# The heads of the mLSTM: spread, logits and denominators' products between the feature tiles of the filling weight products

## The chip, the cores and the metric

The kernel runs on one core of a Trainium2 chip. The metric is the device time of one execution in microseconds; lower is better. The kernel before takes 2386.91 us (median of 3 executions, 2385.71 to 2389.31).

## What is computed

Two transformer blocks over 512 tokens of width 1024, in float32. The first block is a feed-forward part, a mixer, and a feed-forward part. Its mixer projects the normalised input by one weight matrix (29 chunks of 128 output columns here) and feeds two recurrent branches: four heads of a gated linear recurrence (hgrn2) and four heads of the mLSTM. The second block has attention heads in place of the mixer. The change touches only the mLSTM heads, whose reference is (cut):

```
D = where(causal, b[..., :, None] - b[..., None, :] + ic[..., None, :], -inf)
m_t = maximum(a, max(D, axis=-1))
P = einsum("bhtd,bhsd->bhts", qc, kc) * exp(D - m_t[..., None])
num = inter[..., None] * einsum("bhtd,bhdv->bhtv", qc, C) + einsum("bhts,bhsv->bhtv", P, vc)
den = inter * einsum("bhtd,bhd->bht", qc, n) + sum(P, axis=-1)
h = num / maximum(abs(den), exp(-m_t))[..., None]
```

The kernel computes this without chunks: for each head the whole causal half of the 512 x 512 matrix, as ten blocks of 128 x 128 in 1280 columns.

## The kernel before

Every weight chunk (128 x 1024 float32) is loaded by the sync engine's DMA queue into one of three buffers, split by GpSimd into a high and a low part (L323, L325) and multiplied by TensorE: `mm3` (L360 to L362) makes three products of 512 columns (high by high, low by high, high by low), and `pe_dense` (L365) does so for each of the eight feature tiles, 24 products for a chunk, into one bank of PSUM. Each engine runs its own program in order, and semaphores with counts join them.

In the mixer `pe_gated_mixer` writes out TensorE's order by hand. `fill(i)` is one weight chunk; such fills stand between the steps of the recurrences so that TensorE has work while the other engines do theirs. The mLSTM part starts after `fill(23)`. TensorE turns the values (`pe_turn`, L491) into banks 0 to 3, and ScalarE copies these to SBUF (L1337). For each head h there are then:

- `logits(h)`: a spread (L618), which multiplies a selector of 4 rows by the running maximum, 512 columns into bank 3, and four products of keys by queries (L620) with 64 contracted rows and 512, 384, 128 and 256 columns, into banks 0 to 2. The spread releases ScalarE (`decay(h)`, L1351, four exponentials into the buffer E[h % 2]); the last product releases VectorE (`weigh(h)`: L1863 multiplies, L1867 and L1869 mask).
- `values(h)`: waits for the masked E, then four products of values by E (L631, 1280 columns, into bank 6), which VectorE copies out (L1873), and ten products of E by a column of ones for the denominators (L637). After that `den_done` is signalled.
- `pe_head_sums` (L742): four products by a column of ones over the squares that ScalarE makes of the head's output (L1278).

Each float32 product that isn't split into high and low parts shows as two records in the trace, so ten products of denominators are 20 records, four logits are 8.

TensorE's order before is: turn, fill 12, logits 0, fill 13, values 0 (with the denominators), logits 1, fill 14, values 1, sums, logits 2, fill 15, values 2, sums, logits 3, fill 24, values 3, sums, fill 25, sums, fill 26, fill 27, spreads for the norm. A fill waits for ScalarE's copy of the fill two before it (`take`, L1255 and L1257), since two banks alternate. ScalarE's order is: take 12, decay 0, take 13, decay 1, squares, take 14, decay 2, squares, take 15, decay 3, the Silu of the hgrn gate (L1368), take 24, squares, four casts (L1356), squares, takes 25 and 26. VectorE's order is: weigh 0, copy 0, weigh 1, copy 1, weigh 2, copy 2, weigh 3, then the gating of the four hgrn heads (L1841, L1845), copy 3, and the chain of small steps for the denominators and the norm (L1892 and on).

Of the kernel before, what the change touches and what calls it, by code (L numbers as in the profile page):

```python
# [10 lines left out]
ACT = mybir.ActivationFunctionType  # L11
# [3 lines left out]
P = 128  # L15
T = 512
NT = T // P
D = 1024
KD = D // P
# [5 lines left out]
HEADS = 4  # L25
# [20 lines left out]
C_SEL = C_RESET + T  # L46
# [192 lines left out]
def tile(t, i):  # L239
    return t[:, i * T:(i + 1) * T]  # L240
# [46 lines left out]
def fill_bank(tile_number):  # L287
    return 4 + FILL.index(tile_number) % 2
# [75 lines left out]

def pe_dense(k, name, i, bank):  # L365

    pe = k.nc.tensor
    n, hi, lo = k.pair(name, i)
    pe.wait_ge(k.w_split, 2 * n + 2)
    for t in range(KD):  # L370
        m = mm3(pe, k.ps[bank], hi, lo, slice(t * P, (t + 1) * P), tile(k.uhi, t), tile(k.ulo, t), t == 0, t == KD - 1)
    m.then_inc(k.w_used, 1)

# [166 lines left out]
def pe_gated_mixer(k):  # L540
# [7 lines left out]

    def fill(i):
        idx = FILL.index(i)  # L550
        if idx < 2:
            pe.wait_ge(k.qf_taken, 5 + idx)
        else:
            wait_filled(k, pe, FILL[idx - 2])
        pe_dense(k, "mix_in", i, fill_bank(i))

# [49 lines left out]

    def logits(h):

        rows = slice((h % 2) * ML_QK, (h % 2 + 1) * ML_QK)
        qh, kh = tile(g.mqk, h // 2)[rows, :], tile(g.mqk, 2 + h // 2)[rows, :]  # L610
        if h:
            pe.wait_ge(k.decayed, h)
            pe.wait_ge(k.weighed, h)
        else:
            pe.wait_ge(k.turned_copied, 9)
            pe.wait_ge(k.seq_dve, 7)
            pe.wait_ge(k.conv_silu, 1)
        pe.matmul(k.ps[3], k.const[0:HEADS, C_SEL + h * P:C_SEL + (h + 1) * P], g.M, start=True, stop=True).then_inc(k.m_spread, 1)  # L618
        for (i, t0, n, c) in ML_CAUSAL:
            m = pe.matmul(k.psum[:, c:c + n], kh[:, i * P:(i + 1) * P], qh[:, t0:t0 + n], start=True, stop=True)  # L620
        m.then_inc(k.qk_product, 1)

    def values(h):
        E, sum_w = g.E[h % 2], k.ps[7][:, 128:128 + HEADS * NT]
        pe.wait_ge(k.masked, h + 1)
# [7 lines left out]
        m.then_inc(k.hd_out, 1)  # L633
        for j in range(NT):
            for i in range(j + 1):
                c = ML_BASE[i] + (j - i) * P
                m = pe.matmul(sum_w[:, h * NT + j:h * NT + j + 1], E[:, c:c + P], k.cst(C_ONE, 1), start=i == 0, stop=i == j)  # L637
        m.then_inc(k.den_done, 1)

# [57 lines left out]
    pe_turn(k, g.mv_in, 0, 4 * NT)  # L697
    fill(12)
    logits(0)
    fill(13)  # L700
    values(0)
    logits(1)
    fill(14)
    values(1)
    pe_head_sums(k, HEADS)
    logits(2)
    fill(15)
    values(2)
    pe_head_sums(k, HEADS + 1)
    logits(3)  # L710
    fill(24)
    values(3)
    pe_head_sums(k, HEADS + 2)
    fill(25)
    pe_head_sums(k, HEADS + 3)
# [516 lines left out]
def act_gated_mixer(k):  # L1232
    act, g, m = k.nc.scalar, Gated(k), k.misc
    H = HEADS
# [102 lines left out]
    act.copy(g.mv, k.psum[:, 0:4 * T]).then_inc(k.turned_copied, 1)  # L1337
    take(12)

# [18 lines left out]
    decay(0)  # L1358
    take(13)
    decay(1)  # L1360
    squares(H, tile(g.ml_out, 0))
    take(14)
    decay(2)
    squares(H + 1, tile(g.ml_out, 1))
    take(15)
    decay(3)
    act.wait_ge(k.filled, FILL.index(15) + 1)
    act.activation(g.hgate, g.hgate, ACT.Silu).then_inc(k.gates_done, 1)  # L1368
    take(24, ACT.Sigmoid)
    squares(H + 2, tile(g.ml_out, 2))  # L1370
    for h in range(H):
        pair_hi(h, tile(g.hg_out, h))
    squares(H + 3, tile(g.ml_out, 3))
    take(25, ACT.Sigmoid)
    take(26, ACT.Sigmoid)
# [956 lines left out]
```

## Time and profile before

| | |
|---|---|
| median of the runs | 2386.91 us |
| the profiled execution's own time | 2389.54 us |
| its span, first to last instruction | 2387.9 us |
| TensorE matmul busy | 2314.7 us, 97% |
| VectorE / ScalarE / GpSimd busy | 816.6 / 448.7 / 1320.8 us |
| mean granted TensorE clock | 0.986 |

The span is the profiled execution from the first to the last instruction; the 1.6 us between it and the execution's own time lie around it. The granted clock is 1.00 where TensorE runs at 2.4 GHz and 0.50 where it runs at 1.2 GHz. The mLSTM heads lie between 578 and 657 us of the span. A row of the timeline has its start, its duration (a matmul's modelled end lies beyond the start of the next one, so the distance between starts is what counts), engine, line, operation and count.

### The profile page before, as it was taken

The numbers are of one execution on the slowest core, as the hardware profiler recorded it, in microseconds if no ns is written. First come the engines' busy times: TensorE is split into PE (matmuls) and PEld (weight loads), VectorE is DVE, ScalarE is ACT, GpSimd is POOL, SyncE is SP. The second block draws the span as 40 slices with busy tenths as digits, with TensorE's granted clock in tenths as the row PEclk, the third lists the DMA queues.
The fourth block names the chain that finished last, engine by engine and source line by source line (L and its number), as shares of the span: only waits on it lengthen the run. The fifth ranks groups of instructions, "written<-read, shape, count | busy, mean of one in ns | idle before, by whom it ended". The sixth has DMA issues, their size and how long they took to land.

```text
span 2387.9 us, 26080 instructions
## 1 busy us (share of the span) xinstructions
PE 2314.7 (97%) x11060; PEld 1905.6 (80%) x11060; DVE 816.6 (34%) x838; ACT 448.7 (19%) x736; POOL 1320.8 (55%) x772
## 2 busy tenths in 40 slices
PE   6999999999999999999999999999988999999999
PEld 6888888887778888888888888777656788888887
DVE  2323104884244333104323104420567632333013
ACT  3111003323222111003111002111268121111011
POOL 4666665634156666665666665566114656666654
PEclk9999999999799999999999999999899999999999
DMA  4333332211123333332333332223000223333322
GB/s 158 97 97 97 97 97 71 80 54 54 36 80 97 97 97 97 97 97 72 97 97 97 97 97 84 85 88 99 27 1 1 73 86 97 98 97 100 104 86 82
DMA packets 55580, 201.05 MB, mean 84 GB/s; under 512 B 6409, under 2 KB 6537, under 8 KB 55337
## 3 DMA queue, kind: packets, MB, share of 16 engines
q1 hardware_dynamic: 53712, 193.62, 26.4%
q10 hardware_dynamic: 1752, 5.77, 0.6%
q8 instruction: 88, 1.44, 0.3%
q14 instruction: 28, 0.22, 0.0%
HBM read 197.27 MB, written 2.10 MB: 83 GB/s over the span
## 4 chain that ended last, share of the span: by engine, by line
PE 88%; DVE 6%; ACT 3%; issue 1%; DMA 1%; POOL 1%; ACTq 0%; DVEq 0%; POOLq 0%
PE psum L360 19%; PE psum L361 18%; PE psum L362 18%; PE psum L420 7%; PE psum L422 7%; PE psum L421 7%; PE psum L400 1%; PE psum L565 1%; ACT junk L1145 1%; DVE x L1629 1%; PE psum L1069 1%; PE psum L620 1%; PE psum L1071 1%; PE psum L1070 1%; PE psum L458 1%
## 5 line engine op out<-in xcount | busy, mean ns | idle before, releaser
L325 POOL TENSOR_TENSOR w_lo<-w_raw,w_hi 128x1024 fp32r<-128x1024 f32 (+1 forms) x365 | 891.3, 2442 | 30.5
L323 POOL TENSOR_SCALAR w_hi<-w_raw 128x1024 fp32r<-128x1024 f32 (+1 forms) x365 | 388.4, 1064 | 909.9 <-PE psum L362 659.9
L360 PE MATMUL psum<-u_hi,w_hi 128*128 128x512 f32 (+1 forms) x2072 | 795.3, 384 | 10.8 <-DVE work L1977 4.7
L361 PE MATMUL psum<-u_hi,w_lo 128*128 128x512 f32 (+1 forms) x2072 | 789.9, 381 | 0.0
L362 PE MATMUL psum<-u_lo,w_hi 128*128 128x512 f32 (+1 forms) x2072 | 789.4, 381 | 0.0
L360 PEld LDWEIGHTS psum<-u_hi,w_hi 128*128 128x128 f32 x2072 | 392.6, 189 | 90.2 <-issue 7.8
L362 PEld LDWEIGHTS psum<-u_lo,w_hi 128*128 128x128 f32 x2072 | 392.4, 189 | 74.5
L361 PEld LDWEIGHTS psum<-u_hi,w_lo 128*128 128x128 f32 x2072 | 392.8, 190 | 73.6 <-issue 0.7
L420 PE MATMUL psum<-w_hi,hidden_hi 128*128 128x512 f32 x800 | 311.8, 390 | 1.0 <-DVE work L1836 1.0
L421 PE MATMUL psum<-w_lo,hidden_hi 128*128 128x512 f32 x800 | 311.2, 389 | 0.0
L422 PE MATMUL psum<-w_hi,hidden_lo 128*128 128x512 f32 x768 | 298.8, 389 | 0.0
L1666 DVE TENSOR_TENSOR scratch<-scratch,psum 128x512 f32<-128x512 f32 x88 | 60.5, 688 | 586.8 <-PE psum L362 586.8
L1668 DVE TENSOR_TENSOR hidden_lo<-scratch,hidden_hi 128x512 fp32r<-128x512 f32 x88 | 239.4, 2720 | 60.8 <-ACT hidden_hi L1224 60.8
L420 PEld LDWEIGHTS psum<-w_hi,hidden_hi 128*128 128x128 f32 x800 | 150.2, 188 | 32.6 <-DVE work L1836 1.4
L421 PEld LDWEIGHTS psum<-w_lo,hidden_hi 128*128 128x128 f32 x800 | 150.2, 188 | 31.4 <-issue 0.2
L422 PEld LDWEIGHTS psum<-w_hi,hidden_lo 128*128 128x128 f32 x768 | 144.1, 188 | 30.0
L1224 ACT CAST hidden_hi<-scratch 128x512 fp32r<-128x512 f32 x88 | 55.0, 625 | 479.4 <-DVE scratch L1666 479.4
L1222 ACT ACTIVATE scratch<-psum 128x512 f32<-128x512 f32 x88 | 52.6, 598 | 345.9 <-PE psum L362 345.9
L1632 DVE SCALAR_TENSOR_TENSOR x<-psum,x 128x1024 f32<-128x1024 f32 x12 | 14.6, 1218 | 240.2 <-PE psum L422 240.2
L341 POOL TENSOR_SCALAR work<-work,misc 128x512 f32<-128x512 f32 (+3 forms) x32 | 34.2, 1086 | 110.3 <-DVE misc L2109 110.3
L1611 DVE RECIPROCAL misc<-misc 128x1 f32<-128x1 f32 x12 | 1.9, 156 | 243.2 <-ACT misc L1155 243.2
L1145 ACT ACTIVATE junk<-x 128x1024 bf16<-128x1024 f32 x28 | 29.5, 1055 | 272.5 <-DVE x L1632 261.3
(269 smaller groups left out, 1735.6 us busy)
## 6 DMA issues: line engine op xcount, KB each, us to landing
w_raw<-in_ffn_in SPq DMA_DIRECT2D x176, 512.0 KB, 3.5
w_raw<-in_ffn_out SPq DMA_DIRECT2D x88, 512.0 KB, 3.5
w_raw<-in_proj_in SPq DMA_DIRECT2D x34, 512.0 KB, 3.5
w_raw<-in_mix_in SPq DMA_DIRECT2D x29, 512.0 KB, 3.5
w_raw<-in_embed SPq DMA_DIRECT2D x10, 512.0 KB, 3.5
w_raw<-in_mix_out SPq DMA_DIRECT2D x8, 512.0 KB, 3.4
w_raw<-in_branch SPq DMA_DIRECT2D x8, 512.0 KB, 3.6
w_raw<-in_proj_out SPq DMA_DIRECT2D x8, 512.0 KB, 3.5
```

Of the source, the lines that this page charges most:

```text
L323: pool.tensor_scalar(hi, raw, 1.0, 1.0, ALU.mult, ALU.mult).then_inc(k.w_split, 1)
L325: pool.tensor_tensor(lo, raw, hi.bitcast(F32), ALU.subtract).then_inc(k.w_split, 1)
L360: pe.matmul(out, hi[:, cols], xhi, start=first, stop=False)
L361: pe.matmul(out, lo[:, cols], xhi, start=False, stop=False)
L362: return pe.matmul(out, hi[:, cols], xlo, start=False, stop=last)
L420: pe.matmul(bank, xhi(kk)[:, tokens], hi[:, cols], start=kk == 0, stop=False)
L421: pe.matmul(bank, xhi(kk)[:, tokens], lo[:, cols], start=False, stop=False)
L422: return pe.matmul(bank, xlo(kk)[:, tokens], hi[:, cols], start=False, stop=last)
L1145: act.activation(k.junk[:, :], x_tile(k, i), ACT.Square, accum_out=k.x_ss[:, i:i + 1]).then_inc(k.x_squared, 1)
L1224: act.copy(tile(k.hhi, i), hm).then_inc(k.hid_hi, 1)
L1666: dve.tensor_tensor(hm, sg, k.ps[CHUNK_BANK[(2 * i + 1) % 4]], ALU.mult).then_inc(k.multiplied, 1)
L1668: dve.tensor_tensor(tile(k.hlo, i), hm, tile(k.hhi, i).bitcast(F32), ALU.subtract).then_inc(k.hid_lo, 1)
```

## The change

`pe_dense` takes a function that is called after each feature tile but the last. `logits` and the denominators' products are cut up and issued from it: one spread or one product of the logits in a gap, and one column of denominators (1, 2, 3 or 4 products) in a gap. The logits of head h+1 and the denominators of head h now stand in the same fill, logits first. The values' products and the sums stay whole, between fills. Everything moves one fill earlier for the logits: those of head 0 stand in fill 12, not after it.

```
-def pe_dense(k, name, i, bank):
+def pe_dense(k, name, i, bank, between=None):
     for t in range(KD):
         m = mm3(pe, k.ps[bank], hi, lo, slice(t * P, (t + 1) * P), tile(k.uhi, t), tile(k.ulo, t), t == 0, t == KD - 1)
+        if between and t < KD - 1:
+            between(t)

-    def logits(h):
+    def logits(h, t):
-        if h:
-            pe.wait_ge(k.decayed, h)
-            pe.wait_ge(k.weighed, h)
-        else:
-            pe.wait_ge(k.turned_copied, 9)
-            pe.wait_ge(k.seq_dve, 7)
-            pe.wait_ge(k.conv_silu, 1)
-        pe.matmul(k.ps[3], k.const[0:HEADS, C_SEL + h * P:C_SEL + (h + 1) * P], g.M, start=True, stop=True).then_inc(k.m_spread, 1)
+        if t == 0:
+            if h:
+                pe.wait_ge(k.decayed, h)
+                pe.wait_ge(k.weighed, h)
+            else:
+                pe.wait_ge(k.turned_copied, 9)
+                pe.wait_ge(k.seq_dve, 7)
+                pe.wait_ge(k.conv_silu, 1)
+            pe.matmul(k.ps[3], k.const[0:HEADS, C_SEL + h * P:C_SEL + (h + 1) * P], g.M, start=True, stop=True).then_inc(k.m_spread, 1)
-        for (i, t0, n, c) in ML_CAUSAL:
+        elif t <= NT:
+            i, t0, n, c = ML_CAUSAL[t - 1]
             m = pe.matmul(k.psum[:, c:c + n], kh[:, i * P:(i + 1) * P], qh[:, t0:t0 + n], start=True, stop=True)
-        m.then_inc(k.qk_product, 1)
+            if t == NT:
+                m.then_inc(k.qk_product, 1)

+    def denominators(h, j):
...
+        for i in range(j + 1):
+            c = ML_BASE[i] + (j - i) * P
+            m = pe.matmul(sum_w[:, h * NT + j:h * NT + j + 1], E[:, c:c + P], k.cst(C_ONE, 1), start=i == 0, stop=i == j)
+        if j == NT - 1:
+            m.then_inc(k.den_done, 1)
+    def between_heads(h):
+        def between(t):
+            if h + 1 < HEADS and t <= NT:
+                logits(h + 1, t)
+            if t >= 3:
+                denominators(h, t - 3)
+        return between

-    fill(12)
-    logits(0)
-    fill(13)
+    fill(12, lambda t: logits(0, t))
     values(0)
-    logits(1)
-    fill(14)
+    fill(13, between_heads(0))
     values(1)
     pe_head_sums(k, HEADS)
-    logits(2)
-    fill(15)
+    fill(14, between_heads(1))
     values(2)
     pe_head_sums(k, HEADS + 1)
-    logits(3)
-    fill(24)
+    fill(15, between_heads(2))
     values(3)
     pe_head_sums(k, HEADS + 2)
+    fill(24, between_heads(3))
     fill(25)
```

ScalarE's order follows: decay 0, take 12, decay 1, squares, take 13, decay 2, squares, take 14, decay 3, squares, take 15, the gate's Silu, the four casts, squares, take 24, takes 25 and 26. VectorE's and GpSimd's programs are unchanged.

## Rows read from the trace of the kernel before

**Rows 1.** The chain that ended last, by engine (shares of the span).
```profile
PE 88%; DVE 6%; ACT 3%; issue 1%; DMA 1%; POOL 1%; ACTq 0%; DVEq 0%; POOLq 0%
```

**Rows 2.** Windows: stretch, its length, busy us by engine, granted clock, DMA.
```profile
core 0: us, PE busy (x) PEld busy (x) DVE busy (x) ACT busy (x) POOL busy (x), PEclk, DMA share, GB/s
587.20:592.80 5.60, 5.60 (x25) 4.61 (x25) 2.25 (x3) 0.00 (x0) 0.34 (x1) 1.00 0.30 94
597.20:601.90 4.70, 4.70 (x11) 2.18 (x10) 0.00 (x0) 2.30 (x5) 0.00 (x0) 0.71 0.36 112
601.90:609.40 7.50, 7.50 (x26) 6.00 (x25) 2.25 (x3) 0.00 (x0) 0.00 (x0) 0.73 0.00 0
614.70:626.90 12.20, 12.20 (x35) 8.04 (x35) 2.25 (x3) 2.30 (x5) 0.00 (x0) 0.72 0.10 39
632.20:644.40 12.20, 12.20 (x35) 7.90 (x35) 3.46 (x5) 6.26 (x7) 0.00 (x0) 0.72 0.10 39
648.80:656.80 8.00, 8.00 (x33) 6.58 (x34) 3.61 (x7) 1.87 (x3) 0.00 (x0) 0.79 0.23 68
```

**Rows 3.** TensorE in order of time, heads 0 and 1.
```profile
583.51 0.39 PE L362 MATMUL psum<-u_lo,w_hi 128*128 128x512 f32 x1
583.83 1.12 PE L618 MATMUL psum<-work,const 4*128 4x512 f32 x2
584.88 2.42 PE L620 MATMUL psum<-work 64*128 64x512 f32 x8
587.23 0.50 PE L360 MATMUL psum<-u_hi,w_hi 128*128 128x512 f32 x1
587.57 0.40 PE L361 MATMUL psum<-u_hi,w_lo 128*128 128x512 f32 x1
...
592.81 2.32 PE L631 MATMUL psum<-work 128*128 128x512 f32 x8
594.96 2.29 PE L637 MATMUL psum<-const,work 128*128 128x1 f32 x20
597.18 1.12 PE L618 MATMUL psum<-work,const 4*128 4x512 f32 x2
...
601.90 0.79 PE L360 MATMUL psum<-u_hi,w_hi 128*128 128x512 f32 x1
...
609.40 2.32 PE L631 MATMUL psum<-work 128*128 128x512 f32 x8
```

**Rows 4.** TensorE in order of time: a head's sums, and a fill after sums.
```profile
613.71 1.03 PE L742 MATMUL psum<-const,scratch 128*128 128x1 f32 x8
614.67 0.69 PE L618 MATMUL psum<-work,const 4*128 4x512 f32 x1
...
657.63 0.49 PE L360 MATMUL psum<-u_hi,w_hi 128*128 128x512 f32 x1
657.95 0.40 PE L361 MATMUL psum<-u_hi,w_lo 128*128 128x512 f32 x1
```

**Rows 5.** TensorE's weight loads around the logits of head 0.
```profile
583.83 0.29 PEld L618 LDWEIGHTS psum<-work,const 4*128 4x128 f32 x2 [0.35 <-issue]
587.23 0.19 PEld L360 LDWEIGHTS psum<-u_hi,w_hi 128*128 128x128 f32 x1 [0.33 <-issue]
```

**Rows 6.** The turned values: TensorE's first product of fill 12, ScalarE's copy.
```profile
578.18 0.48 PE L360 MATMUL psum<-u_hi,w_hi 128*128 128x512 f32 x1
578.47 1.87 ACT L1337 COPY work<-psum 128x2048 f32<-128x2048 f32 x1 [2.12 <-PE psum L491]
```

**Rows 7.** VectorE's weighing of head 0: first and last operation.
```profile
587.42 1.49 DVE L1863 SCALAR_TENSOR_TENSOR work<-work,psum 128x1280 f32<-128x1280 f32 x1 [16.39 <-PE psum L620]
589.42 0.28 DVE L1869 TENSOR_TENSOR work<-work,const 128x128 f32<-128x128 f32 x1
```

**Rows 8.** ScalarE's Silu of the gate, VectorE from the first hgrn remainder to the last head's copy.
```profile
636.43 1.91 ACT L1368 ACTIVATE work<-work 128x2048 f32<-128x2048 f32 x1
646.30 2.50 DVE L1845 TENSOR_TENSOR hidden_hi<-work,hidden_hi 128x512 fp32r<-128x512 f32 x1 [4.88 <-ACT hidden_hi L1356]
651.13 0.68 DVE L1873 COPY work<-psum 128x512 f32<-128x512 f32 x1
```

More of the change, by code:

```diff
@@ L547, in pe_gated_mixer, with fill @@
         pe_dense(k, "mix_in", FIRST[n], CHUNK_BANK[n % 4])
-    def fill(i):
+    def fill(i, between=None):
         idx = FILL.index(i)
@@ L554, in fill @@
             wait_filled(k, pe, FILL[idx - 2])
-        pe_dense(k, "mix_in", i, fill_bank(i))
+        pe_dense(k, "mix_in", i, fill_bank(i), between)
     def level(n):
@@ L605, in hgrn_out @@
         m.then_inc(k.hd_out, 1)
-    def logits(h):
+    def logits(h, t):
         rows = slice((h % 2) * ML_QK, (h % 2 + 1) * ML_QK)
         qh, kh = tile(g.mqk, h // 2)[rows, :], tile(g.mqk, 2 + h // 2)[rows, :]
-        if h:
-            pe.wait_ge(k.decayed, h)
-            pe.wait_ge(k.weighed, h)
-        else:
-            pe.wait_ge(k.turned_copied, 9)
-            pe.wait_ge(k.seq_dve, 7)
-            pe.wait_ge(k.conv_silu, 1)
-        pe.matmul(k.ps[3], k.const[0:HEADS, C_SEL + h * P:C_SEL + (h + 1) * P], g.M, start=True, stop=True).then_inc(k.m_spread, 1)
-        for (i, t0, n, c) in ML_CAUSAL:
+        if t == 0:
[9 more added lines that the diff above has]
+            i, t0, n, c = ML_CAUSAL[t - 1]
             m = pe.matmul(k.psum[:, c:c + n], kh[:, i * P:(i + 1) * P], qh[:, t0:t0 + n], start=True, stop=True)
-        m.then_inc(k.qk_product, 1)
+            if t == NT:
+                m.then_inc(k.qk_product, 1)
     def values(h):
-        E, sum_w = g.E[h % 2], k.ps[7][:, 128:128 + HEADS * NT]
+        E = g.E[h % 2]
         pe.wait_ge(k.masked, h + 1)
@@ L633, in values @@
         m.then_inc(k.hd_out, 1)
[L634 to L638, printed above, removed]
+    def denominators(h, j):
+        E, sum_w = g.E[h % 2], k.ps[7][:, 128:128 + HEADS * NT]
+        for i in range(j + 1):
[10 more added lines that the diff above has]
+        return between
     def rows():
@@ L1337, in act_gated_mixer @@
     act.copy(g.mv, k.psum[:, 0:4 * T]).then_inc(k.turned_copied, 1)
-    take(12)
     act.wait_ge(k.cols_done, 1)
@@ L1358, in act_gated_mixer @@
     decay(0)
-    take(13)
+    take(12)
     decay(1)
     squares(H, tile(g.ml_out, 0))
-    take(14)
+    take(13)
     decay(2)
     squares(H + 1, tile(g.ml_out, 1))
+    take(14)
+    decay(3)
+    squares(H + 2, tile(g.ml_out, 2))
     take(15)
-    decay(3)
     act.wait_ge(k.filled, FILL.index(15) + 1)
     act.activation(g.hgate, g.hgate, ACT.Silu).then_inc(k.gates_done, 1)
-    take(24, ACT.Sigmoid)
-    squares(H + 2, tile(g.ml_out, 2))
     for h in range(H):
@@ L1373, in act_gated_mixer @@
     squares(H + 3, tile(g.ml_out, 3))
+    take(24, ACT.Sigmoid)
     take(25, ACT.Sigmoid)
```

## The prediction

> **What bounds the kernel now.** I read the chain of waits first. TensorE holds 88% of it [rows 1], so nearly all time is TensorE's, and a change of its order counts fully where it never idles. The question is then what its time in this stage is made of. I listed its timeline from the turn of the values (578 us) to the last sums (657 us): it has no idle time there, every row starts where the one before ends [rows 3]. So neither ScalarE nor VectorE sets the pace, and nothing that they do sooner brings anything. Then I asked for the granted clock of each stretch [rows 2]. This is what the reader is to see: fill 13 runs at 1.00 and takes 5.6 us, but logits 1 run at 0.71 and fill 14 at 0.73, the stretches of heads 2 and 3 at 0.72, and fill 25 with the sums before it at 0.79. The clock sits at 1.2 GHz in part of each, without any idle time of TensorE. What ran before each fall is alike: the denominators' products (one moving column each), the sums (one column), the spread (4 rows) and the start of the logits (64 rows), in one unbroken piece. After logits 0, which stand alone between two fills, it does not fall.
>
> **The gain: the clock.** Logits and fill at full clock are head 0's: from the spread at 583.83 to the values at 592.81, 8.98 us. Head 1's, from 597.18 to 609.40, are 12.22 us [rows 3]. That costs 3.24 us. By the clock alone it would be 4.7 x 0.29 + 7.5 x 0.27 = 3.39 us [rows 2]; the real loss is 0.956 of it. Over all six stretches: 1.36 + 2.03 + 12.2 x 0.28 x 2 + 8.0 x 0.21 = 11.9 us [rows 2], times 0.956 is **11.4 us**. That is all that a steady clock can give.
>
> Will the clock hold? In the new order the longest piece without a wide product of 128 rows is the sums (0.96 us [rows 4]) and then, after a tile of 0.68 us, the spread; every other narrow piece is at most a 512-column product of logits or 0.9 us of denominators, with 0.68 us of weight product on either side. In the old order denominators, sums, spread and the first logits ran together before the falls in heads 2 and 3, 2.22 + 0.96 + 1.05 us and more [rows 3, 4]. Around logits 0, with a fill on either side of 3.4 us of spread and logits, no fall came. I take it that the clock holds in the heads, with some doubt, since wide products fill only 5.45 of each 11 to 12 us.
>
> **The price: changes of rows.** The weight loads show it [rows 5]. Before a product with 4 or 64 rows after one of 128, and before one of 128 after one of 64, the load starts only when the array is free: 0.35 and 0.33 us without a load, and the load and its product start together. In numbers [rows 3]: 1280 columns of values with 128 rows take 594.96 - 592.81 = 2.15 us, the same 1280 columns of logits take 587.23 - 584.88 = 2.35, so 0.20 more. The spread's 512 columns should be 0.86 and take 1.05, 0.19 more. Going in costs 0.09 (583.51 + 0.227 = 583.74, start at 583.83), and the fill's first product after it takes 0.34, not 0.227, 0.11 more. Altogether 0.09 + 0.19 + 0.20 + 0.11 = 0.59 us for three changes, 0.20 each. Before there are three changes in a head: fill to spread, spread to logits, logits to fill. After there are ten, two around each of the five single pieces. Seven more, in four heads, 28 x 0.20 = **5.6 us**. (A fill's ordinary pace of 0.227 is fill 13: 24 products in 5.58 us less 0.12 for its slow start.)
>
> The Trainium skill says (TensorE: Matmul & The Clock Gate, Part 3, The mechanism) that TensorE pulls a weight load ahead of running products when its row group doesn't conflict or it goes into the background buffer. By that, the loads between changes of rows should mostly hide. The trace shows them hidden from 128 rows to 128 rows only [rows 5]; by the rule the 5.6 us would be near nothing, and the forecast some 5 us lower. I follow the rows; the rule is a rival below.
>
> **The price: denominators in pieces.** A one-column product costs its weight load, 2.22 us for 20 = 0.111 each [rows 3]; that stays, wherever it stands. But after the last the fill's load has nothing to hide under: the first product of a fill after sums takes 0.32 us, not 0.227 [rows 4], so 0.10. Before, denominators were followed by other narrow work. Now there are 16 pieces, and two more sums go straight into a fill: 18 x 0.10 = 1.8 us, with a little at the entry **2.0 us**. Bounds: nothing, if the load hides, and 18 x 0.2 = 3.6, if it is priced as a change of rows.
>
> **The waits.** (1) The spread of head 0 waits for ScalarE's copy of the turned values, which ends at 578.47 + 1.87 = 580.34 [rows 6]. Before, all of fill 12 lay over it. Now only the first tile does: from 578.18 three products, to about 578.97. With 0.1 us to the release the spread starts near 580.45, so TensorE idles **1.4 us**, with the other seven tiles queued behind it. Its own other conditions are long met. (2) Values 0 wait for the mask. From the first operation of weighing to the end of the last, 587.42 to 589.70 [rows 7], and 0.27 us before it from the last logits' stream end (587.15): 2.55 us, 2.65 with the release. After the last logits piece there are three tiles, 0.09 + 0.34 + 8 x 0.227 = 2.25 us. **0.4 us** idle; before, a whole fill covered it. For heads 1 to 3 the three tiles have denominators 1 (part), 2 and 3 between them, 1.5 us more, and it is covered. (3) The idle 1.4 us stands between the turn, one tile and the narrow spread. A fall of the clock there would cost like fill 25's, 8.0 x 0.21 x 0.956 = 1.6 us [rows 2]; I give it a half: **0.8 us**. Bounds for (1): 0.9 to 2, by what the release costs; for (2) 0 to 1.
>
> **Costed at nothing.** The decay of a head follows its spread by the same distance, and the weighing waits for the last logits anyway. Take 12 behind decay 0 is late by nothing, as fill 14 needs it only a head later. The Silu now starts after take 15, that is after fill 15: about 0.8 + 1.28 (table load, the time from the decay's end to 636.43) + 1.91 = 4 us after it [rows 8]. Then VectorE has the gating and the copy of head 3: two operations of 0.68 us and what took from 646.30 to 651.81 [rows 8], 6.9 us, and ScalarE's squares 0.6: about 12 us after fill 15. The last sums, before fill 26, come after values 3 (2.15), sums (0.96), fill 24 with denominators (5.45 + 2.2 + 0.5) and fill 25 (5.45), some 17 us after it. Slack 5 us, and if it were gone it would be paid one for one. The weights come with the same order of chunks and more time between them. What follows (root, diagonals, spreads, output products) hangs on fills 26 and 27 as before and moves with them.
>
> **The sum.** -11.4 + 5.6 + 2.0 + 1.4 + 0.4 + 0.8 = -1.2 us. On the profiled execution: 2389.54 - 1.2 = 2388.3. This one execution lies 2.6 us above the median 2386.91, so the forecast in medians is **2385.7, say 2386 us**: a large gain eaten nearly whole. Its own range, by the bounds of the terms, is 2383 to 2389.
>
> **Rivals.**
>
> *A, the clock still falls in the heads.* Wide products fill only about half of each fill now. Against it: around logits 0 the mix was the same and the clock held. For it: here the sums stand right before it, and such a mix goes on for 30 us on end. If it falls as often as before, the gain is nothing and all prices stay: -0 + 7.6 + 1.8 + 0.8 = +10, 2397 us. If it falls once or twice, at 1.6 to 3.3 us each, 2387 to 2392. The point from which it decides against the change is at about one fall of 1.6 us above my sum. This is the one on the slower side.
>
> *B, the changes of rows hide.* This is what the rule in the Trainium skill (the page and section above) would make of it. Then 28 changes cost nothing, -11.4 + 2.0 + 2.6 = -6.8, 2380 us. Every change of rows in this stretch speaks against it [rows 5].
>
> *C, another engine is late for the new order.* VectorE's gating collides with GpSimd's split, as at 646.30, where a remainder took 2.50 us in place of 0.68 [rows 8], and copy 3 is late for the last sums. It would need 5 us of it, three collisions: 2388 to 2391.
>
> **How the numbers follow.** My forecast 0.58; A in full 0.06, A in part 0.18; B 0.12; C 0.06. Runs of this kernel are told apart at about 0.2%, 4.8 us, so faster is below 2382.1 and slower above 2391.7. Faster: B and a little of my own case, 0.14. Slower: A in full, a third of A in part, some of C, 0.16. The rest, 0.70, is no change. The range 2381 to 2392 leaves out A in full and part of B.
>
> **What would show it.** Right: the granted clock at 1.00 through fills 13 to 25, with at most one short fall at fill 12. In each gap a weight load of L618, L620 that begins with its product, and a fill's first product at about 0.34 us after it. An idle row of 1.4 us before L618 of head 0, released by ScalarE L1337, and 0.4 us before L631 of head 0, released by VectorE. TensorE's time from the turn's end to the end of the last sums, 79.45 us before (578.18 to 657.63 [rows 6, 4]), is then about 78. Wrong: a clock of 0.5 in fills 13 to 15, loads hidden at changes of rows, or idle rows before L742.

## The result and the profile after

The changed kernel takes **2407.06 us** (median of 11 executions, 2387.03 to 2417.31), the kernel before 2386.9 (11 executions, 2385.71 to 2390.41). The ratio is 1.0072, with a 95% interval of 1.0051 to 1.0092: slower by 0.7%. The forecast was 2386, with a range of 2381 to 2392. More telling than the median is the spread: 30 us, where the kernel before has 5.

The traced execution took 2393.86 us (span 2392.2), so it is one of the quicker ones. The mean granted clock of every execution tells the rest: at 2387.03 us it is 0.989, at 2417.31 us 0.975. The time at 1.2 GHz is the time x (1 - clock) x 2, as the clock has two levels: 52.5 us in the one, 120.9 in the other. 68 us more at the low clock cost 30.3 us, 0.44 us each, near what the traces give below. So the clock explains most of the spread, but not all of it: two executions with a mean clock of 0.989 took 2387.03 and 2394.5 us, and the kernel before varies from 2385.0 to 2391.1 us at an unchanged 0.986 (the executions beside after_spread128). What those 6 to 8 us are no run here shows.

The chain of waits is TensorE's as before (that row was [rows 1]):
```profile
PE 88%; DVE 6%; ACT 4%; issue 1%; DMA 1%; POOL 1%; ACTq 0%; DVEq 0%; POOLq 0%
```

Stretches of the changed kernel, with the columns of [rows 2]: a low stretch in fill 12, fill 13, a low stretch, fill 14 up to values 2, and fill 15.
```profile
582.90:589.70 6.80, 6.80 (x14) 3.35 (x13) 0.00 (x0) 0.00 (x0) 0.00 (x0) 0.50 0.00 0
595.10:608.00 12.90, 12.90 (x58) 7.95 (x57) 2.94 (x4) 2.30 (x5) 1.29 (x1) 1.00 0.14 42
613.70:634.10 20.40, 20.40 (x50) 12.69 (x50) 2.25 (x3) 2.17 (x5) 1.37 (x2) 0.50 0.05 19
611.00:632.30 21.30, 21.30 (x56) 13.12 (x57) 2.28 (x4) 2.30 (x5) 0.80 (x1) 0.56 0.08 25
636.20:649.00 12.80, 12.80 (x55) 7.89 (x56) 2.30 (x4) 2.30 (x5) 0.00 (x0) 1.00 0.12 42
```
Fills 13 and 15 have the same pieces as fill 14 and take 12.9 and 12.8 us at full clock; fill 14 takes 21.3, as the clock falls near its start and does not come back in it. In the kernel before, the three falls in heads 1 to 3 lasted 6.8 us each and ended in the whole fill behind them; this is the first, which began in logits 1 and ended in fill 14:
```profile
599.20:606.00 6.80, 6.80 (x17) 4.66 (x16) 2.25 (x3) 1.44 (x4) 0.00 (x0) 0.50 0.03 12
```

TensorE in fill 12, and around the long fall (idle time ahead of a row and its releaser in brackets):
```profile
577.62 0.48 PE L360 MATMUL psum<-u_hi,w_hi 128*128 128x512 f32 x1
579.82 1.12 PE L621 MATMUL psum<-work,const 4*128 4x512 f32 x2 [1.26 <-ACT work L1351]
...
595.67 0.40 PE L362 MATMUL psum<-u_lo,w_hi 128*128 128x512 f32 x1
595.99 1.12 PE L621 MATMUL psum<-work,const 4*128 4x512 f32 x2
597.04 0.51 PE L360 MATMUL psum<-u_hi,w_hi 128*128 128x512 f32 x1
597.38 0.40 PE L361 MATMUL psum<-u_hi,w_lo 128*128 128x512 f32 x1
...
610.14 0.95 PE L756 MATMUL psum<-const,scratch 128*128 128x1 f32 x8
610.96 0.48 PE L360 MATMUL psum<-u_hi,w_hi 128*128 128x512 f32 x1
611.83 1.12 PE L621 MATMUL psum<-work,const 4*128 4x512 f32 x2
612.88 0.50 PE L360 MATMUL psum<-u_hi,w_hi 128*128 128x512 f32 x1
613.82 2.07 PE L624 MATMUL psum<-work 64*128 64x512 f32 x2
...
632.28 3.24 PE L636 MATMUL psum<-work 128*128 128x512 f32 x8
635.36 0.95 PE L756 MATMUL psum<-const,scratch 128*128 128x1 f32 x8
```
The reader is to see three things. The spread of head 0 waits 1.26 us for ScalarE's copy, as forecast (1.4). The fall at 613.7 stands behind sums, one tile, the spread and one tile. It ends within values 2, and the sums of 635.36 run at full pace again (0.82 us to the next fill at 636.17): the last tile and the values are the first products of this stretch that are 128 rows wide for 3 us on end. The third is the price of a piece at full clock: from the last wide product at 595.67 to the second one after the spread, 597.38, there are 1.71 us, of which 0.227 + 0.227 are the two wide products and 0.86 the spread's columns: 0.40 for two changes of rows, as forecast.

From the turn to the end of the last sums TensorE takes 88.5 us (577.62 to 666.14), 79.45 before. To compare orders without the clock I take off 0.478 us for each microsecond at 1.2 GHz in this stage (a wide product takes 0.427 us there and 0.227 at 2.4 GHz, so 1 - 0.227/0.427 would be 0.468; with the narrow products at one half, 0.478 is between). This is an estimate from the trace, called "at full clock" below: 79.45 - 0.478 x 23.9 = **68.0** before, 88.5 - 0.478 x 27.3 = **75.5** after. It can be checked in one place: dense_pass_again, below, ran the changed order without a fall in 92.5 us, and less its 16.4 us of added work that is 76.1. So a microsecond at the low clock cost (88.5 - 76.1)/27.3 = 0.45 us in the new order, and the estimate is 0.6 us too low for the changed kernel. The new order costs 7.5 to 8.1 us by itself, and the low clock, which was to go, is as long in this execution as before, and up to 68 us longer in others, over the whole kernel. (The stage is 9.1 us longer and the span only 4.3. Outside the stage this execution has 32.8 us at the low clock and that of before 46.4, which makes 6.5 of it; the remaining 1.7 us are not accounted for.) Outside the stage the traces of all kernels have 32.8 to 63.5 us at the low clock, so of the 120.9 us of the slowest execution at least 57 lie in the stage, twice what the traced one had.

### The profile page after: what moved, and what is told of

Same layout as the page of the kernel before. It is cut to its first block, busy times and chain, and to the rows that moved or that the text cites. A ratio compares the mean times of both kernels' runs of the same rounds, so it can differ in the third digit from the quotient of the medians.

```text
span 2392.2 us, 26080 instructions
## 1 busy us (share of the span) xinstructions
PE 2318.8 (97%) x11060; PEld 1901.0 (79%) x11060; DVE 812.9 (34%) x838; ACT 448.5 (19%) x736; POOL 1320.1 (55%) x772
## 4 chain that ended last, share of the span: by engine, by line
PE 88%; DVE 6%; ACT 4%; issue 1%; DMA 1%; POOL 1%; ACTq 0%; DVEq 0%; POOLq 0%
PE psum L360 19%; PE psum L362 18%; PE psum L361 18%; PE psum L422 7%; PE psum L424 7%; PE psum L423 7%; PE psum L402 1%; ACT junk L1159 1%; DVE x L1643 1%; PE psum L567 1%; PE psum L624 1%; PE psum L1083 1%; PE psum L1084 1%; PE psum L1085 1%; PE psum L460 1%
## 5 line engine op out<-in xcount | busy, mean ns | idle before, releaser
L1159 ACT ACTIVATE junk<-x 128x1024 bf16<-128x1024 f32 x28 | 29.5, 1055 | 272.5 <-DVE x L1646 261.3
```

The costliest lines, as they stand in the source:

```text
L1159: act.activation(k.junk[:, :], x_tile(k, i), ACT.Square, accum_out=k.x_ss[:, i:i + 1]).then_inc(k.x_squared, 1)
```

## The experiments

Theory 1 holds that a low clock keeps itself in fills with narrow pieces: wide 128-row work between them is too thin to bring 2.4 GHz back. (Taken strictly it is refuted below; as a tendency it stands.) Theory 2, its rival, changes with the experiment; in each the expectation names it. All the kernels below were timed beside the kernel before, whose median was 2385.9 to 2387.9 us in all of these comparisons. Each median is of 4 (logits_in_gaps) to 12 executions.

Stage is the time from the turn to the end of the last sums in the traced execution. The last figure, at full clock, is the estimate by 0.478, and too low where the new order fell for long: by 0.6 and 0.8 us for the changed kernel's two traces, and at 0.45 us in place of 0.478 by some 1.8 for logits_in_gaps.

| kernel | median us | lowest to highest | ratio, 95% interval | stage us, low us in it, at full clock |
|---|---|---|---|---|
| logits_in_gaps | 2413.75 | 2409.01 to 2415.28 | 1.0107, 1.0094 to 1.0121 | 104.9, 64.9, 73.9 |
| denominators_in_gaps | 2376.83 | 2375.44 to 2380.9 | 0.9959, 0.9947 to 0.9972 | 70.0, 3.4, 68.3 |
| after_rows128 | 2377.23 | 2372.23 to 2382.21 | 0.9959, 0.9946 to 0.9972 | 68.6, 0, 68.6 |
| before_rows128 | 2382.81 | 2371.58 to 2387.58 | 0.9972, 0.996 to 0.9985 | 75.9, 20.5, 66.1 |
| dense_pass_again | 2407.22 | 2397.64 to 2413.17 | 1.0086, 1.0066 to 1.0106 | 92.5, 0, 92.5 |
| head0_two_gaps_later | 2388.78 | 2382.59 to 2399.15 | 1.002, 1.0003 to 1.0037 | 80.0, 3.4, 78.4 |
| spread_alone_logits_whole | 2376.89 | 2374.33 to 2379.73 | 0.996, 0.9948 to 0.9972 | 68.8, 0, 68.8 |
| after_again | 2400.08 | 2387.42 to 2416.89 | 1.0072, 1.0041 to 1.0104 | 80.2, 10.2, 75.3 |
| denominators_and_sums_in_gaps | 2381.32 | 2376.75 to 2383.32 | 0.9974, 0.9964 to 0.9985 | 71.3, 5.7, 68.6 |
| sums_alone_in_gap | 2386.74 | 2382.25 to 2389.18 | 0.9997, 0.9988 to 1.0005 | 77.9, 20.5, 68.1 |
| sums_in_gap | 2397.78 | 2390.58 to 2400.46 | 1.0032, 1.002 to 1.0044 | 85.1, 20.5, 75.3 |
| head0_later_and_sums_in_gap | 2392.52 | 2388.13 to 2399.95 | 1.0028, 1.0016 to 1.004 | 84.9, 13.7, 78.3 |
| after_spread128 | 2383.8 | 2378.6 to 2388.05 | 0.9988, 0.998 to 0.9997 | 74.7, 0, 74.7 |
| pieces_in_two_gaps | 2391.64 | 2387.22 to 2401.15 | 1.0018, 1.0007 to 1.0028 | 80.9, 20.5, 71.1 |
| sums_in_own_gap | 2378.64 | 2372.78 to 2382.82 | 0.9961, 0.9948 to 0.9975 | 70.3, 3.4, 68.7 |

### One part alone: logits, or denominators

logits_in_gaps (the changed kernel, where `between_heads` issues the logits alone; head 0's lines, the others alike):
```
     values(0)
+    for j in range(NT):
+        denominators(0, j)
     fill(13, between_heads(0))
```


> The changed kernel with the denominators' products whole behind the values again; only spread and logits stand in the gaps. Theory 1 (the low clock holds itself): once TensorE is at 1.2 GHz, a fill with narrow pieces in it does not bring 2.4 GHz back, only mostly wide 128-row work does. The denominators and sums before each fill make it fall in every head, and fills 13 to 15 stay low nearly whole: TensorE's time from the turn to the last sums about 100 us in place of 79.5, so 2400 to 2412 us, with little spread since it happens every time. Theory 2 (each fall ends after some 7 us as in the kernel before, and the idle 1.3 us in fill 12 starts the long ones): the falls cost 11 us as before, the changes of rows 5.7 and the waits 1.5, so about 2394, or the same spread as the changed kernel.

2413.75 us, all four executions above 2409: 2 us over theory 1's range of 2400 to 2412, and far from theory 2's 2394. The traced execution (2415.28 us, mean clock 0.975) is like the slowest of the changed kernel, and its only idle row in the stage is the 1.26 us in fill 12. The stretches at the low clock, in the traced execution:
```profile
582.40:596.10 13.70, 13.70 (x26) 7.25 (x26) 2.25 (x3) 1.12 (x4) 0.00 (x0) 0.50 0.00 1
602.90:620.00 17.10, 17.10 (x32) 8.74 (x32) 2.25 (x3) 2.73 (x6) 1.34 (x2) 0.50 0.01 6
626.80:640.40 13.60, 13.60 (x26) 6.80 (x25) 2.25 (x3) 1.82 (x5) 0.00 (x0) 0.50 0.00 0
647.30:664.40 17.10, 17.10 (x31) 8.38 (x31) 2.25 (x3) 2.30 (x5) 0.00 (x0) 0.50 0.02 9
```
Four falls of 13.6 to 17.1 us, one in each fill with pieces, and a fifth of 3.4 us in fill 25. Those of fills 13 to 15 start at the spread or just behind it, after the denominators and one tile; in the kernel before the falls start at the same kind of place. Here each lasts twice as long or more; the one in fill 12 has no counterpart there.

denominators_in_gaps (the kernel before with the denominators alone in the gaps; fills 15, 24 and 25 likewise):
```
-    fill(14)
+    fill(14, between_heads(0))
```


> The kernel before with one edit: the denominators' products stand in gaps of the next fill; spread and logits are whole and stand between fills as before. Theory 1 (the low clock holds itself where narrow pieces are dense enough): denominators are only 2.2 us of 7.7 us of a fill, so fills stay mostly wide and each fall ends within 7 us as before; the fall in fill 25 goes (-1.6 us), 16 exposed weight loads cost 1.6: 2384 to 2390 with a spread under 5 us. Theory 2 (any piece in the gaps keeps the clock low): 2395 to 2415 with a spread of 20 us.

2376.83 us, faster than the kernel before by 9.6 us (2386.47 beside it), and 7 us below theory 1's range. Windows from fill 14 to the last sums; only one short stretch is low, and none is before them:
```profile
597.00:612.00 15.00, 15.00 (x73) 11.21 (x74) 3.52 (x5) 2.89 (x6) 3.39 (x2) 1.00 0.18 59
612.00:625.00 13.00, 13.00 (x66) 9.76 (x65) 2.36 (x4) 2.30 (x5) 3.39 (x2) 1.00 0.09 17
625.30:628.70 3.40, 3.40 (x9) 2.39 (x8) 2.62 (x4) 3.37 (x3) 0.00 (x0) 0.50 0.14 58
628.70:646.00 17.30, 17.30 (x101) 14.69 (x100) 7.04 (x9) 4.92 (x9) 3.41 (x2) 1.00 0.10 31
```
So the gain that the change was worth is real, and the denominators carry it. I had taken it that the falls of heads 1 to 3 would stay; all but one short one went.

### Rows

after_rows128 and before_rows128:
```
-        qh, kh = tile(g.mqk, h // 2)[rows, :], tile(g.mqk, 2 + h // 2)[rows, :]
+        qh, kh = tile(g.mqk, h // 2), tile(g.mqk, 2 + h // 2)
-            pe.matmul(k.ps[3], k.const[0:HEADS, C_SEL + h * P:C_SEL + (h + 1) * P], g.M, start=True, stop=True).then_inc(k.m_spread, 1)
+            pe.matmul(k.ps[3], k.const[:, C_SEL + h * P:C_SEL + (h + 1) * P], tile(g.mqk, 0), start=True, stop=True).then_inc(k.m_spread, 1)
```


> The changed kernel, but spread and logits contract over 128 rows (the spread reads queries in place of the running maximum, the logits add two heads, so the mixer's output is another one). Same records, columns, order and waits. Theory 1: no change of rows is left (-40 x 0.2 = -8 us against the changed kernel at full clock) and the pieces no longer look idle to the clock, so it holds in the heads: about 2378 us, spread under 5 us. Theory 2 (the idle wait in fill 12 and the one-column products make the long falls, rows do not matter): the clock falls as in the changed kernel, 2380 to 2408 us with a spread of 20 us.

> The kernel before, but spread and logits contract over 128 rows (another output of the mixer, same columns, order and waits). Theory 1: the falls of heads 1 to 3 came because spread and logits with 4 and 64 rows followed the denominators; with 128 rows they end the quiet piece, so most of the 10 us of heads 1 to 3 is given back, and 12 changes of rows at 0.2 us go: 2373 to 2378 us. Theory 2 (one-column products alone make the fall): falls as before, only the 2.4 us of the changes go, 2384 us.

The first did what theory 1 said: 2377.2 us and no low stretch in the heads, though with a spread of 10 us (said: under 5). The second did not: 2382.8 us, not 2373 to 2378, and three falls of 6.8 us remain in the traced execution. What TensorE did ahead of the first, and the windows of two of them:
```profile
605.16 2.32 PE L631 MATMUL psum<-work 128*128 128x512 f32 x8
607.31 2.29 PE L637 MATMUL psum<-const,work 128*128 128x1 f32 x20
609.46 1.71 PE L742 MATMUL psum<-const,scratch 128*128 128x1 f32 x8
```
```profile
609.60:616.50 6.90, 6.90 (x17) 4.23 (x18) 0.00 (x0) 2.30 (x5) 0.00 (x0) 0.51 0.25 76
626.70:633.50 6.80, 6.80 (x18) 4.13 (x18) 0.00 (x0) 3.19 (x6) 0.00 (x0) 0.50 0.27 77
```
With full rows in spread and logits the clock still falls as the denominators end and the sums begin: one-column products alone are quiet enough. In the kernel before, then, narrow rows were not needed for the fall, but they made it surer: three of the 11 executions with full rows have a mean clock of 0.992, while the kernel before beside them had 0.986 to 0.988 in all 15. In the changed kernel the narrow rows are needed (after_spread128 below). One rival stays open: the kernels with full rows also multiply other numbers. In before_rows128 they did not keep the clock up; apart from the rows they were not tested in the new order.

The pair also prices the pieces. At full clock the stage is 66.1 us with the old order and 68.6 with the new, of which 1.64 are waits (1.26 and 0.39), so cutting 128-row work into pieces costs 0.8 us. With narrow rows it is 68.0 and 75.5, with 1.45 of waits: 6.0 (6.6 by the 76.1 of dense_pass_again, with its 1.42 of waits). The 28 further changes of rows cost the difference, 5.2 to 5.8 us, **about 0.2 each**.

### Does wide work end a fall?

dense_pass_again (`again` is set for fills 13, 14 and 15):
```
+    if again:
+        for t in range(KD):
+            m = mm3(pe, k.ps[bank], hi, lo, slice(t * P, (t + 1) * P), tile(k.uhi, t), tile(k.ulo, t), t == 0, t == KD - 1)
```


> The changed kernel, and behind fills 13, 14 and 15 their 24 wide products are made a second time without pieces (start flag set again, so the output is the same). That is 3 x 5.45 = 16.4 us more work at full clock. Theory 1 (the low clock holds itself in fills with pieces, and only wide work ends it): every fall now ends in the next second pass, so the spread of the runs shrinks from 30 us to under 12 and the time is 2387 + 16.4 + at most three falls of 5 us: 2403 to 2418 us, no run above 2420; no stretch at 1.2 GHz longer than 14 us. Theory 2 (the length of a fall is chance or set by something off TensorE): 16.4 us on top of the changed kernel's distribution: median 2423, runs from 2403 to 2434.

2407.22 us, against 2400.08 for the changed kernel beside it (after_again): 7 us more for 16.4 us more work, though with six and seven executions and such spreads the 7 is rough. The highest execution, 2413.17, is below the changed kernel's 2416.89, and its time at the low clock, 72.4 us by the mean clock, is far below the 120.8 there. The traced one ran this stage without a fall, in fill 12 too, which the edit does not touch, so the trace by itself doesn't show that the wide passes end falls:
```profile
577.60:670.00 92.40, 90.98 (x403) 62.73 (x401) 16.66 (x24) 21.58 (x34) 18.68 (x12) 1.00 0.10 32
```
The spread of 15.5 us is more than the 12 said, and half of the changed kernel's. That neither the median of 2423 nor the 2434 of theory 2 came speaks for theory 1: about half of the added wide work or more was paid for by the clock.

pieces_in_two_gaps:
```
-            if h + 1 < HEADS and t <= NT:
-                logits(h + 1, t)
-            if t >= 3:
-                denominators(h, t - 3)
+            if t == 3 and h + 1 < HEADS:
+                for n in range(NT + 1):
+                    logits(h + 1, n)
+            if t == 6:
+                for j in range(NT):
+                    denominators(h, j)
```


> The changed kernel, but in fills 13 to 15 the spread and all logits stand together in the gap behind the fourth tile, all denominators together behind the seventh (also in fill 24); head 0 in fill 12 as in the changed kernel. 18 changes of rows fewer. Theory 1 (scattered pieces hold a low clock, a run of wide tiles ends it): falls may still start behind spread and logits, but each ends in the next four tiles, so none is longer than 14 us: 2380 to 2393 us, none above 2400. Theory 2 (where the pieces stand does not matter, their sum in a fill does): as the changed kernel less 3 us, 2384 to 2412 us.

2391.64 us, with all but one of 11 executions under 2395 and one at 2401.15, where I had said none above 2400. The median lies in the ranges of both theories; it is the spread, 14 us where the changed kernel has 30, that speaks for the first. In the trace the pieces of fills 13 to 15 left two falls of 3.4 us; the long one, 13.6 us, is in fill 12, where head 0's pieces are still scattered:
```profile
582.70:596.30 13.60, 13.60 (x26) 7.22 (x26) 2.25 (x3) 1.03 (x3) 0.00 (x0) 0.50 0.00 0
```
But the order does not settle how long a fall lasts. Fill 12 has the same pieces in the changed kernel, here, in logits_in_gaps and in sums_in_gap. Its fall lasted 13.6 us in the last three and 10.2 in after_again, and ended behind 2.5 to 3.5 us of wide products; in the changed kernel's first trace (582.90 above) it lasted 6.8 us and ended among the pieces, ahead of the last of the logits. This is after_again:
```profile
583.35:593.59 10.24, 10.24 (x21) 5.55 (x21) 2.25 (x3) 0.00 (x0) 0.00 (x0) 0.50 0.00 0
```
So wide work between pieces can bring 2.4 GHz back; it does so late and not every time.

### What starts a fall in the new order?

after_spread128 is the changed kernel with the second pair of lines of the diff above alone.

> The changed kernel with only the spread over 128 rows (it reads queries in place of the running maximum, so the mixer's output is another one); logits keep 64 rows, order and waits stay, the idle 1.26 us in fill 12 too. Theory 1 (quiet work by rows starts the falls): 8 changes of rows go (-1.4 us) and the quiet pieces beside sums and idle time are gone, so nearly no fall from fill 12 to 25: 2383 to 2389 us, none above 2395. Theory 2 (idle time and one-column products start them, whatever the rows): spread of the changed kernel, 2386 to 2415 us.

No execution above 2388.05, a spread of 9 us, and the whole stage at full clock, idle wait in fill 12 and all:
```profile
576.20:650.90 74.70, 73.28 (x332) 49.85 (x330) 16.67 (x24) 21.68 (x34) 18.78 (x12) 1.00 0.13 40
```
By the mean clock no execution had more than 57.3 us low in the whole kernel, and the traced one had all its low stretches outside the stage; 14 of the changed kernel's 18 executions had more. The four spreads of 4 rows, 1.05 us each, are the piece without which its long falls were not seen, and the idle wait alone did not start one.

head0_two_gaps_later:
```
-    fill(12, lambda t: logits(0, t))
+    fill(12, lambda t: logits(0, t - 2) if t >= 2 else None)
```


> The changed kernel, with head 0's spread and logits two gaps later in fill 12, so that ScalarE's copy of the turned values is done when the spread comes. Theory 1: the idle 1.26 us goes, but values 0 wait 1.4 us longer for the mask (one tile stands behind the last logits in place of three), so the sum stays; the fall at fill 12 becomes rarer, and the long falls in fills 13 to 15 stay, as they start at the sums and spreads there: 2385 to 2417 us with a median of 2395 to 2408. Theory 2 (the idle time in fill 12 is what starts the long falls): they go, 2384 to 2388 us with a spread under 5 us.

2388.78 us, in two clusters (seven executions from 2382.6 to 2389.5, five from 2397.9 to 2399.2). That is between the theories. None of 12 is above 2400, where the changed kernel had 10 of its 18, which points to fill 12 as the start of the longest executions. The slow cluster still has 34 us more at the low clock than the fast one (mean clocks 0.985 and 0.992). The wait for the mask was not 1.6 us, as I had said, but 4.01. VectorE, GpSimd and TensorE there:
```profile
587.99 0.87 DVE L1881 TENSOR_TENSOR work<-work,const 128x384 f32<-128x384 f32 x1
588.78 2.42 DVE L1883 TENSOR_TENSOR work<-work,const 128x128 f32<-128x128 f32 x1
```
```profile
587.41 1.04 POOL L323 TENSOR_SCALAR w_hi<-w_raw 128x1024 fp32r<-128x1024 f32 x1 [9.73 <-PE psum L362]
588.54 2.52 POOL L325 TENSOR_TENSOR w_lo<-w_raw,w_hi 128x1024 fp32r<-128x1024 f32 x1
```
```profile
591.26 1.22 PE L636 MATMUL psum<-work 128*128 128x512 f32 x1 [4.01 <-DVE work L1883]
```
The last mask takes 2.42 us in place of 0.28 [rows 7], and ends 0.14 us after GpSimd's split. The end of fill 12 had released that split. This is rival C's collision, at a place where I had not looked.

sums_in_gap and head0_later_and_sums_in_gap (the first is this diff, the second adds the one above):
```
             if t >= 3:
                 denominators(h, t - 3)
+            if h and t == 6:
+                pe_head_sums(k, HEADS + h - 1)
```


> The changed kernel with only the sums moved into the last gap of the fill, so that no fill starts behind them. Theory 1: in the profile of the changed kernel the 20 us fall began behind values, sums, one tile and the spread of head 2; with the sums gone from there fewer falls start in fills 14 and 15, but one that starts at fill 12 is still held through fill 13: 2385 to 2412 us, median near 2392. Theory 2 (the idle 1.26 us in fill 12 is what starts them): as the changed kernel, median above 2400, highest above 2412.

> The changed kernel with both edits, head 0's pieces two gaps later and the sums in the last gap. Both theories: neither start of a fall is left, so the clock holds from fill 12 to 25 in nearly every run: 2382 to 2386 us with a spread under 5 us. That is the changed kernel with its prices (40 changes of rows, 12 of them there before, and the wait for the mask) and without its falls, and is to be compared with denominators_in_gaps at 2377: the difference is what the single pieces of spread and logits cost at full clock, 5.7 us for 28 changes of rows by my rows, and about 1.4 us more wait.

sums_in_gap took 2397.78 us, in theory 1's range but 6 us above its median of 2392, and below the 2400 of theory 2. Its trace has the long fall of 13.6 us in fill 12, and two of 3.4 us each in fills 14 and 15 where the changed kernel had one of 20.5. The second kernel was to be free of falls at 2382 to 2386 and took 2392.52. Two things that I had built in fit it: the 4.01 us wait stands there too (78.3 us at full clock, not 75.5), and in gap 6 the longest denominators piece and the sums now make one quiet piece of 1.8 us. Two of its three low stretches, the first from the end of the wait through the values, the second behind such a piece:
```profile
592.40:599.20 6.80, 6.17 (x12) 3.61 (x13) 1.27 (x2) 0.00 (x0) 0.43 (x1) 0.50 0.22 77
626.50:630.00 3.50, 3.50 (x7) 1.75 (x6) 0.00 (x0) 0.59 (x1) 2.45 (x2) 0.51 0.00 0
```

### The sums, in the good order

denominators_and_sums_in_gaps is denominators_in_gaps with the same three lines; sums_in_own_gap moves its denominators to gaps 0 to 3 (`if t <= 3: denominators(h, t)`); sums_alone_in_gap is the kernel before with the sums in gap 6 and nothing else.

> denominators_in_gaps with one more edit: the sums of heads 4 to 6 stand in the last gap of the next fill, no longer right before spread and logits. Theory 1 (the clock falls behind quiet work in one piece, and holds where it is broken up): the one short fall left in the profile of denominators_in_gaps, behind sums, spread and logits 3, goes: 1.6 us less and 0.3 us more for exposed loads, so about 1 us below it, 2375 to 2376 us, spread under 5 us. Theory 2 (the denominators alone made the falls): as denominators_in_gaps, 2377 us.

> denominators_and_sums_in_gaps with the denominators in the first four gaps, so that the sums have the last gap to themselves. Theory 1 (1.8 us quiet in one piece was what cost there): no fall in the heads in most runs, 2375 to 2377.5 us, under both denominators_in_gaps_and_sums (2381.3) and at or under denominators_in_gaps (2376.8). Theory 2 (sums in a gap are dear in themselves): 2380 to 2383 us.

> The kernel before with only the sums moved into the last gap of the next fill; denominators, spread and logits whole as before. Theory 1: denominators 2.2, spread 1.05 and the first logits still run in one piece before each fill, so the falls of heads 1 to 3 stay, each of 7 us, at most a little rarer; the one in fill 25 may go: 2383 to 2387 us. Theory 2 (the sums tip it over): the falls go, 2376 to 2379 us.

denominators_and_sums_in_gaps took 2381.3 us, against both theories; beside the kernel before it is 0.9974 (0.9964 to 0.9985), where without the sums moved it was 0.9959 (0.9947 to 0.9972), so it is at best no better. TensorE at its fall at 620.1, behind the piece of denominators and sums:
```profile
618.46 0.95 PE L645 MATMUL psum<-const,work 128*128 128x1 f32 x8
619.27 1.09 PE L761 MATMUL psum<-const,scratch 128*128 128x1 f32 x8
620.22 0.78 PE L360 MATMUL psum<-u_hi,w_hi 128*128 128x512 f32 x1
```
Apart, in sums_in_own_gap, they give 2378.6 (2372.8 to 2382.8), above the 2375 to 2377.5 of theory 1 and below the 2380 of theory 2. The intervals of these three kernels overlap, and what the joined piece costs stays open. sums_alone_in_gap changes nothing (0.9997, 20.5 us low in its stage): the denominators, and not the sums, start the falls of the kernel before.

### A whole order from what was learnt

spread_alone_logits_whole: denominators in gaps 0 to 2, the spread of the next head but one in gap 4, the sums in gap 6, the four logits products whole behind the values.
```
+            if t in (0, 1):
+                denominators(h, 3 - t)
+            elif t == 2:
+                denominators(h, 1)
+                denominators(h, 0)
+            elif t == 4 and h + 2 < HEADS:
+                logits(h + 2, 0)
+            elif t == 6:
+                pe_head_sums(k, HEADS + h)
```


> A new order: denominators in the first three gaps of the next fill, the spread alone in a gap of the fill before its logits, the four logits products whole behind the values, the head's sums in the last gap. Theory 1: no two quiet pieces meet and each fill is mostly wide, so the clock never falls from fill 12 to 25. Against the kernel before: -11.4 for the clock, +0.9 for one more change of rows pair in four heads less one, +1.2 for 12 exposed loads, +0.3 for sums: 2378 us, spread under 3 us; perhaps 1 us below denominators_in_gaps. Theory 2 (pieces in gaps are dear in themselves): above denominators_in_gaps, 2380 us or more, since there is one more piece in each fill.

2376.89 us, no low stretch in the stage, spread 5.4 us; as denominators_in_gaps, not better. Both beat the kernel before by 0.4%, and this one beats the changed kernel by 1.0% (after_again, beside it).

> The changed kernel once more, for a second profile and its spread beside the others on one chip. Theory 1: runs differ by how long the clock stays at 1.2 GHz in fills 12 to 24, 7 to 50 us of it, nothing else in the stage differs: 2387 to 2418 us, and where the profile's time is above 2400, the low stretches in this stage add up to over 35 us. Theory 2 (something else, a DMA or an engine, is late in the slow executions): idle rows of TensorE above 2 us in the stage.

The changed kernel again had a spread of 29.5 us; its profile fell on one of its best (2387.42), with one low stretch of 10.2 us in the stage and 75.3 us at full clock, 0.2 from the first. There is no trace of an execution above 2400 us of this very kernel, so neither theory was put to its test; for those the mean clock speaks (0.975 at 2416.9 us), and the trace of logits_in_gaps.

## Why the prediction was wrong

**The step that failed** is "Will the clock hold? ... I take it that the clock holds in the heads". It rested on two places: no fall after logits 0, and the falls behind denominators, sums, spread and logits in one piece. From that I drew that breaking the piece up would do. It does for the denominators (denominators_in_gaps, 3.4 us low in place of 23.9), not for spread and logits: the spread of 4 rows beside sums or idle time still starts falls (after_spread128 has none). In place of the steady clock behind the -11.4 us, the stage had 27.3 us at 1.2 GHz in the traced execution and at least 57 in the slowest. Logits 0 were not "the same mix": they stood as one piece of 3.4 us between two whole fills.

**Rival A was the right one and priced too low.** I let it cost at most what the old falls had cost, 2397 us, "if it falls as often as before", and gave it 0.06 in full. I missed that a fall has an end as well as a start. The whole fills of the kernel before ended each within 6.8 us; the changed kernel took just those away. Its falls last 6.8 and 20.5 us in the trace, 13.6 to 17.1 in logits_in_gaps, and by the mean clock there are up to 68 us more in all. The rows were there to be read: by [rows 2] fill 14 ran at 0.73, so the clock came back within its wide products, and there are few such products on end in the new order. That it is their absence which makes falls long fits dense_pass_again and pieces_in_two_gaps, but no run isolates it, and one fall of the changed kernel ended without them.

**The gain** of 11.4 us for a steady clock was sized about right. That the estimate goes from 79.45 to 68.0 is no proof, as its 0.478 is half of the prediction's 0.956. But spread_alone_logits_whole, with no low stretch, has a stage of 68.8 us, 10.6 less than before and with the price of its own pieces in it, and denominators_in_gaps took 9.6 in the median.

**The prices.** Changes of rows: 5.6 us forecast, 5.2 to 5.8 by the two pairs. Pieces of denominators: 2.0 forecast, 0.8 by the pair with full rows and 0.3 in denominators_in_gaps (68.3 for 68.0), within the bounds. Waits: 1.26 for the copy (1.4 forecast) and 0.19 for the mask (0.4). Together 7.5 to 8.1 for 9.4. The rule of the Trainium skill (TensorE: Matmul & The Clock Gate, Part 3, The mechanism), by which loads should hide, didn't hold across changes of rows here, as the rows before had shown; rival B is out.

**Rival C**, the collision of VectorE and GpSimd, was not seen in the changed kernel. It is real where head 0 stands two gaps later: 2.1 us on the mask. Its price was not worked out in the prediction: three collisions of 1.8 us are 5.5 us, which the slack of 5 us would nearly have taken, not 2 to 5 us on top.

**Silu and the end of the stage** cost nothing, as forecast: there is no idle row before the last sums. The sum at full clock would have been 2386.9 - 11.4 + 7.5 = 2383, or 2384 with 8.1; the traced execution of 2387.42 still had 10.2 us low in the stage.

## What to carry to other kernels

Where the granted clock has fallen, look in the profile for what ended the fall as well as for what began it, and be slow to cut up the stretch of wide products that ended it. Spread out work that is quiet by columns (one-column products, 0.11 us each here wherever they stand); keep work of few rows in one piece, since each change between 4, 64 and 128 rows costs about 0.2 us of TensorE. Judge such an order by the spread and the mean clock of ten executions: a profile of one tells little of it.

## What the runs showed of the hardware

- Falls are a matter of the execution: the same program had a mean clock of 0.989 and of 0.975, with 2387 and 2417 us.
- One-column products of 128 rows behind each other (2.15 us of denominators as the sums begin) are enough for a fall, even where the next work is 128 rows wide (before_rows128), though TensorE is busy all the time.
- Mixed work that does not make the clock fall may yet fail to bring it back: fills 13 and 15 ran at 1.00 with the pieces with which fill 14 stayed at 0.50. It is not certain either way: the fall in fill 12 lasted 6.8, 10.2 and 13.6 us with the same pieces.
- A change between 128 rows and 4 or 64 cost about 0.2 us of TensorE, as the weight load behind it was not hidden (5.2 to 5.8 us for 28 changes).
- A VectorE mask of 128 columns took 2.42 us in place of 0.28 beside GpSimd's split of a weight chunk.
